# A block with attention, a recurrence, cross-attention and retrieved experts: the last 128 tokens go ahead of the other 384

## The reference

```python
h = rms_norm(x, norm1_g)
qa, ka, va, xl, gl, qc = split(h @ w_in)
o_a = chunk_band_attention(...); o_b = rg_lru_branch(...); o_c = memory_cross_attention(...)
g = sigmoid(h @ w_gate + b_gate)                    # three gates of 2048
x = x + (g0 * (o_a @ wA) + g1 * (o_b @ wB) + g2 * (o_c @ wC)) @ w_o
h = rms_norm(x, norm2_g)
# PEER: 8 heads, each 2 x 128 keys, top 16 of each side, top 16 of the 256 sums
q = h @ w_peer_q;  idx, g = route(q, peer_keys)     # 128 of 16384 experts a token
x = x + sum_k g_k * gelu(peer_u[idx_k] . h) * peer_v[idx_k]
```

## Time and profile before

| | |
|---|---|
| median of 3 runs | 3796.72 us (3788.9 to 3797.24) |
| span of the profiled execution | 3795.8 us (no other time of it is given) |
| TensorE busy | 3763.3 us, 99% |
| VectorE, GpSimd, ScalarE busy | 2360.2, 1701.2, 1259.6 us |
| moved by DMA | 801.10 MB, mean 211 GB/s |

### The profile page before, as it was taken

How to read it: one execution, slowest core, us unless ns; L and a number is a source line. 1 busy time by engine, 2 the same in 40 slices (tenths; PEclk the granted TensorE clock), 3 DMA queues, 4 the chain that set the end, 5 groups by cost and what they waited for, 6 DMA issues and landing times.

```text
span 3795.8 us, 56588 instructions
## 1 busy us (share of the span) xinstructions
PE 3763.3 (99%) x20213; PEld 3454.6 (91%) x20213; DVE 2360.2 (62%) x4031; ACT 1259.6 (33%) x1640; POOL 1701.2 (45%) x1453
## 2 busy tenths in 40 slices
PE   8999999999999999999999999999999999999999
PEld 6778778888888888889999999999999999999999
DVE  5482453000000207886978878888888888888887
ACT  3433453333333323224642222222232222222222
POOL 1444334444444663444025455555544555554222
PEclk9999999999999999999999999999999999999999
DMA  6222112222222323334579889889988898889786
GB/s 209 89 89 101 66 67 89 99 99 92 96 99 99 134 99 109 106 107 147 225 306 328 314 316 343 317 314 335 328 292 294 325 327 312 306 326 338 277 295 226
DMA packets 187962, 801.10 MB, mean 211 GB/s; under 512 B 21024, under 2 KB 59944, under 8 KB 134440
## 3 DMA queue, kind: packets, MB, share of 16 engines
q1 hardware_dynamic: 100864, 492.61, 35.9%
q0 software_dynamic: 83840, 303.09, 22.5%
q10 hardware_dynamic: 3128, 3.88, 0.5%
HBM read 762.39 MB, written 37.09 MB: 211 GB/s over the span
## 4 chain that ended last, share of the span: by engine, by line
PE 88%; DMA 5%; DVE 3%; issue 3%; POOL 1%; ACT 0%; DVEq 0%; POOLq 0%; SPq 0%; ACTq 0%
PE bank L1805 87%; DMA grow<-v_rows,g_col 3%; DMA grow<-u_rows,g_col 2%; DVE w_lo L1625 1%; DVE g_acc L1660 1%; DVE grow L1653 0%; POOL grow L776 0%; DVE xT L1679 0%; DMA ring<-w_exp 0%; PE bank L1982 0%; DMA arena<-mem_t 0%; DVE act_in L1632 0%; DVE act_hi L1636 0%; ACT w_hi L807 0%; POOL w_lo L738 0%
## 5 line engine op out<-in xcount | busy, mean ns | idle before, releaser
L807 ACT ACTIVATE w_hi<-ring 128x1024 fp32r<-128x1024 f32 (+1 forms) x499 | 564.2, 1136 | 1132.8 <-PE bank L1805 612.9
L647 POOL TENSOR_TENSOR p_lo<-ring,p_hi 128x512 fp32r<-128x512 f32 x432 | 563.4, 1305 | 667.4 <-ACT p_hi L807 588.8
L1805 PE MATMUL bank<-h_hi,w_hi 128*128 128x368 f32 (+1 forms) x2304 | 779.9, 338 | 4.7 <-DVE w_lo L1625 3.1
L1805 PE MATMUL bank<-h_hi,w_lo 128*128 128x368 f32 (+1 forms) x2304 | 773.7, 336 | 0.0
L1805 PE MATMUL bank<-h_lo,w_hi 128*128 128x368 f32 (+1 forms) x2304 | 770.8, 336 | 0.0
L1805 PE MATMUL bank<-act_hi,w_hi 128*128 128x368 f32 x2048 | 673.8, 329 | 3.4 <-DVE xT L1679 3.4
L1805 PE MATMUL bank<-act_lo,w_hi 128*128 128x368 f32 x2048 | 673.5, 329 | 0.0
L1805 PE MATMUL bank<-act_hi,w_lo 128*128 128x368 f32 x2048 | 673.5, 329 | 0.0
L776 POOL DMA_INDIRECT grow<-v_rows,g_col x288 | 378.2, 1313 | 537.1 <-DVE g_acc L1660 367.9
L776 POOL DMA_INDIRECT grow<-u_rows,g_col x288 | 365.9, 1270 | 561.4 <-DVE grow L1653 263.4
L1625 DVE TENSOR_TENSOR w_lo<-ring,w_hi 128x1024 fp32r<-128x1024 f32 x448 | 546.4, 1220 | 70.7 <-ACT w_hi L807 47.8
(11 more groups left out here) (226 smaller groups left out, 5077.5 us busy)
## 6 DMA issues: line engine op xcount, KB each, us to landing
ring<-w_exp SPq DMA_DIRECT2D x256, 1024.0 KB
ring<-w_mix SPq DMA_DIRECT2D x64, 1024.0 KB, 4.9
tables<-wt SPq DMA_DIRECT2D x12, 2048.0 KB, 6.5
wg<-tables SPq DMA_DIRECT2D x96, 256.0 KB
ring<-w_qk SPq DMA_DIRECT2D x20, 1024.0 KB, 4.9
ring<-w_o SPq DMA_DIRECT2D x16, 1024.0 KB, 4.8
ring<-w_pq SPq DMA_DIRECT2D x16, 1024.0 KB
xT<-x_t SPq DMA_DIRECT2D x8, 1024.0 KB, 11.9
```

Of the source, the lines that this page charges most:

```text
L647: nc.gpsimd.tensor_tensor(p_lo[:, part, :], ring[slot][:, part, :], p_hi[:, part, :].bitcast(F32), ALU.subtract).then_inc(quarter_lo, 1)
L807: return nc.scalar.activation(out, in_, func, **kw)
L1805: return nc.tensor.matmul(out, lhsT, rhs, start=start, stop=stop)
```

## The change

`NX` goes from 16 to 64, so `ND` from 368 to 320, and the tables from 11 and a half to 10 blocks. The last 128 tokens ("a") go through gates, branch products, merge, output product, second norm, queries, scores and routing first, in 96 parts of 1 MB (64 + 16 + 16), with the tokens as the stationary side and 512 output columns of weights as the moving one. A part is 12 matmuls. Its load takes 2 KB from each row of four tiles. After them the other 384 tokens go through the same weights again, in tiles of 8 KB a row as before, with matmuls of 384 columns. The routing of the early tokens is ranked on VectorE during the first 12 of these tiles; then 110 rows of `u` are gathered beside the tiles (one or two a tile), and 10 more beside the `u` tiles before the tables. In that stage the low parts of quarters 0 and 1 are made by GpSimd and 2 and 3 by VectorE. The rest of the 192 `u` rows and the 192 `v` rows are gathered in the long loop and the tail.

```diff
-NX = 16
+NX = 64
-NTB = TM // TB
+NTB = ND // TB
+A_MIX, A_WO, A_PQ = 64, 16, 16
+A_ALL = A_MIX + A_WO + A_PQ
+QUIET = 12
+B_ROWS = tuple(0 if m < QUIET or m in (63, 64) else 1 if m % 3 == 1 else 2 for m in range(MIX_TILES + KC))
+U1_ROWS = (0, 0, 0, 2, 2, 2, 2, 2)
+U_ROWS = 20
+V_ROWS = 19
...
 SP, before the second pass:
+            def quarter_of(a):
+                part, i = slice(S * (a % 4), S * (a % 4) + S), a // 4
+                if a < A_MIX:
+                    src = mix_of[4 * (i // 4):4 * (i // 4) + 4, i % 4, :, part]
+                else:
+                    w, i = (w_o, i - A_MIX // 4) if a < A_MIX + A_WO else (w_pq, i - (A_MIX + A_WO) // 4)
+                    src = w[4 * i:4 * i + 4, :, part]
+                return src.rearrange("t p n -> p t n")
+            for a in range(A_ALL):
...
+                    sync.wait_ge(a_low, 2 * (a - 2))
+                    sync.wait_ge(a_last, a - 2)
+                sync.dma_start(a_raw[a % 3]..., quarter_of(a)).then_inc(slot_in[a % 3], 16)
...
 ScalarE:
+            def a_high_part(a):
+                act_e.wait_ge(slot_in[a % 3], RINGS + 16 * (a // 3 + 1))
...
+                    act_e.wait_ge(a_done, a - 1)
+                for half in range(2):
+                    part = slice(2 * half, 2 * half + 2)
+                    f(a_hi[a % 2][:, part, :]..., src[:, part]).then_inc(a_high, 1)
...
 VectorE:
+            def a_low_part(a):
+                dve.wait_ge(a_high, 2 * a + 1)
+                v.tensor_tensor(lo[:, 0:2], raw[:, 0:2], hi[:, 0:2].bitcast(F32), ALU.subtract).then_inc(a_low, 1)
+                dve.wait_ge(a_high, 2 * a + 2)
+                v.tensor_tensor(lo[:, 2], raw[:, 2], hi[:, 2].bitcast(F32), ALU.subtract).then_inc(a_low, 1)
...
 GpSimd: the last quarter of each part; then, in the second pass:
+            def early_rows(begin, count):
+                for i in range(begin, begin + count):
+                    for half in range(2):
+                        to = 2 * (i % 2) + half
+                        pool.wait_ge(gath_free, 2 * i + half + 1)
+                        pool.indirect_dma_start(grow[to][:, :], None, half_rows[0],
+                                                bass.IndirectOffsetOnAxis(g_both[:, i, half:half + 1], 0)).then_inc(gath_in[to], 16)
+            for m in range(MIX_TILES + KC):
+                low_quarters(m)
+                if m + 1 < len(B_ROWS):
+                    early_rows(sum(B_ROWS[:m + 1]), B_ROWS[m + 1])
...
+            for j in range(JG):
+                low(R_U1 + j, j % 2)
+                early_rows(N_B + sum(U1_ROWS[:j]), U1_ROWS[j])
...
+            pool.wait_ge(tab_mm, TAB_PARTS)
+            gather_all(0, half_rows[0], g_both, PAIRS, x_both, N_EARLY // 4)
...
 TensorE:
+            def a_part(a, out, of_hi, of_lo, first=0, last=KC - 1, closes=True):
+                for c in range(4):
+                    if c == 0:
+                        pe.wait_ge(a_low, 2 * a + 1)
+                    elif c == 2:
+                        pe.wait_ge(a_low, 2 * a + 2)
+                    elif c == 3:
+                        pe.wait_ge(a_last, a + 1)
+                    k = 4 * (a % 4) + c
+                    ins = split_mm(out, of_hi(k), of_lo(k), a_hi[a % 2][:, c, :], a_lo[a % 2][:, c, :],
+                                   k == first, closes and k == last)
+                ins.then_inc(a_done, 1)
...
+                for t in range(4):       # the bias of a gate, by a diagonal
+                    ins = mm(bank[b][:, P * t:P * t + P], ones[:, :], bias_d[i % 2][:, t, :], start=False, stop=t == 3)
...
-                    ins = split_mm(bank[3 + b][:, :], p_hi[:, n, :], p_lo[:, n, :], branch_hi[n], branch_lo[n],
+                    ins = split_mm(bank[3 + b][:, 0:TM], p_hi[:, n, :], p_lo[:, n, :], mix_hi_b[:, n, :], branch_lo[n][:, 0:TM],
```

More of the change, by code:

```diff
@@ L86 @@
 R_DVE = R_TAB + 1
[L87 removed]
+X_AFTER, EXP_AFTER, ROUTE_AFTER = 5, 5, 6
 BANK_U = (2, 3)
@@ L239, in hybrid_block @@
[L239 to L246, removed]
+        wg = [place("wg", 168, [NTB, JG * TB])[:, :, :], place("wg2", 112, [NTB, JG * TB])[:, :, :]]
+        grow = [place(f"grow{i}", row_at[i], [D // 2]) for i in range(4)]
@@ L687, in _ @@
             fill_low(0)
-            pool.wait_ge(at_a.scores, TT)
+            pool.wait_ge(heads.scores, TT)
             q_stage(2)
@@ new lines, in _ @@
+            for j in range(2):
+                top_pair(j)
+            merge(0)
+            for j in range(2, 4):
+                top_pair(j)
+            row_index()
+            shift_scores()
+            merge(1)
+            dve.wait_ge(tok_copied, 4)
+            done = 0
+            for m in range(QUIET, MIX_TILES):
+                low_quarter(m, 2)
+                first = done
+                if B_ROWS[m]:
+                    a_u_row(done)
+                low_quarter(m, 3)
+                if B_ROWS[m] == 2:
+                    a_u_row(done + 1)
+                done += B_ROWS[m]
+                if m % 4 == 1:
+                    merge((m - 5) // 4)
+                if m == QUIET + 6:
+                    share_scores()
@@ new lines, in _ @@
+            for c in range(KC - 1):
+                merged_low(c)
+            low_quarter(MIX_TILES, 2)
+            merge(KC - 1)
+            low_quarter(MIX_TILES, 3)
+            merged_low(KC - 1)
+            for k in range(1, KC):
+                m = MIX_TILES + k
+                low_quarter(m, 2)
+                if B_ROWS[m]:
+                    a_u_row(done)
+                low_quarter(m, 3)
+                if B_ROWS[m] == 2:
+                    a_u_row(done + 1)
+                done += B_ROWS[m]
+                if k >= 2:
+                    add_x(k - 2)
+                    square(k - 2)
@@ new lines, in _ @@
+            dve.wait_ge(const_made, 4)
+            for q in range(1, 4):
+                part = slice(4 * q, 4 * q + 4)
+                if q < 3:
+                    dve.wait_ge(third_hi, q + 1)
+                else:
+                    dve.wait_ge(split_hi, 3)
+                    dve.wait_ge(second_lo, 4)
+                v.tensor_tensor(w_lo[0][:, part, :], ring[0][:, part, :], w_hi[0][:, part, :].bitcast(F32), ALU.subtract
+                                ).then_inc(third_lo if q < 3 else split_lo, 1)
@@ L2196, in _, with tables @@
             pe.wait_ge(route_copied, 3)
-            def tables(t, b, first, parts=4):
+            def tables(t, b, first):
                 n = 2 * t + b + R_TAB
```

1176 lines of the change are left out of this document (736 added, 440 removed).

## The result

| | before | after |
|---|---|---|
| median | 3794.72 us (3788.9 to 3797.24) | 3887.5 us (3886.38 to 3891.4) |
| ratio, 95% interval | 1 | 1.0247 [1.0233, 1.0262] |
| profiled span | 3795.8 us | 3885.5 us |

The change makes the kernel 2.5% slower; 3692 us were forecast. L numbers are now lines of the changed kernel (and in the experiments lines of each one's own).

The account below looks back on a forecast made before the run. TensorE, busy 99% of the span, was taken as the bound. -244.5 + 15.8 + 5.2 + 37 + 28 + 8 + 20 - 1.1 + 25 + 2 = -104.6 us gave 3692 us, 2.8% faster; 8-in-10 range 3625 to 3800.

Parts of the forecast that it names:

- Dense experts: 256 tiles of 48 matmuls, narrowed from 368 to 320 columns; each matmul saves 19.9 ns: -244.5 us.
- The loop: Long loop of 12 groups of 16 tiles: 2% of 1350 us lost under heavier load, +25 us (0 to +90).
- Rival B: Long loop: VectorE and the gathers become the bound, tiles of 7.4 to 7.7 us, about 3750 to 3810 us; chance 12%.
- Two passes: Gates, output and query products: same columns, but 1,152 more matmuls each paying the rest of 13 ns: +15.8 us.
- First pass at 3.1 us a part: 96 parts of the early tokens, paced nearest to the round of three load buffers: +37 us (bounds +4 and +210).
- Rival C: First pass starves: loads of 2 KB runs at half rate, 5.35 us a part, +216 us, 3908 us; chance 12%.
- Serial places: First pass: start, norm before queries, last merge and change back to tiles, with slow clock after each: +28 us (15 to 45).
- Rival D: First pass: the clock falls to 1.2 GHz, 5.1 us a part, +190 us, 3885 us; chance 3%.
- Second pass beside the rows: 110 row gathers beside tiles of 8.29 us: all engines fit, GpSimd barely, +8 us (0 to +50).
- Rival E: Second pass: GpSimd is late, 68 tiles at 9.0 us, +48 us, 3740 us; chance 5%.
- Eight expert tiles before the tables: The u tiles there: GpSimd's splits stand behind gather issues in five tiles, plus lost clock: +20 us (5 to 30).
- Tables: Table stage: VectorE sets 15.0 us a block; 10 blocks and 6 plain tiles of 7.0 us after: -1.1 us.

Follow-up runs that it names:

- the kernel with the second row later: Changed kernel with nearer gate-weight blocks, VectorE alone on first-pass low parts and early merge; GpSimd issues each tile's second row behind that tile's quarters: 3773.8 us, ratio 0.9955.

## Why the prediction was wrong, point by point

The span rose by 89.7 us where -104.6 was the sum: a miss of 194 us.

- **Dense experts, -244.5: right.** 684 matmuls in 100 us are the 146.2 ns forecast.
- **The loop, +25, and the tail, +2: wrong by 14 us together, in the kernel's favour.** 10,317 matmuls in 1530 us at 146.2 ns are 1508 us, so 22 us were lost in loop and tail; but the kernel before had already lost 15 in 1460, and the +25 was to come on top. From the first matmul of the loop to that of the tail it took 1546.3 us before and 1353.6 after: 192.7 less, where the narrower matmuls alone give 183.4, so the +25 was -9. Tail and end gave back 8 us of the 29 forecast. Rival B didn't come: VectorE 88% and 334 GB/s over the stretch were carried.
- **Two passes, +15.8: right.** Without rows the second pass has 8.34 us a tile against 8.29. The small matmuls, +5.2, were not priced by any run.
- **First pass at 3.1 us a part, +37: wrong by 76 us.** With the serial places it was to last 96 x 3.1 + 28 = 326 us; from its first matmul to that of the second pass it took 402 us (566 to 968). The step that failed is "the DMA engines carried 393 GB/s ... where most packets were under 2 KB": it looked at the size of the pieces and not at where they lie. 44 us come back with nearer blocks. Another 35 come back with VectorE alone on the splits: "VectorE 1.22 and about 0.65 us, and one GpSimd quarter of 1.31 us" were taken as durations side by side, and they lengthen each other. With both edits the marks show 3.20 us a part, and the pass takes 323 us. Rival C had the place, and its threshold (4.2 us a part) was passed by a little, at 4.33 and not at its 5.35; the reason that it gives, short pieces, was not it. The paragraph on the 4 MB between the blocks points to the same rival, at half the rate (196 GB/s); 237 were measured.
- **Serial places, +28: not separable,** but in line with those 323 us. Rival D didn't come: the clock was 0.95 in 600 to 700 us.
- **Second pass beside the rows, +8 (0 to 50): wrong by 120 us,** the largest error. From 968 to 1759 us it took 791 us for 80 tiles, forecast 671; without the rows 121 us come back. The step that failed is "All fit, GpSimd barely ... so a tile can lend to the next". I added each engine's work and compared sums. But the work is in order, and each row ties the engines: GpSimd's quarters stand behind issues that wait for VectorE's products, these stand behind quarters of VectorE's that wait for GpSimd's. Take away either the products or the transfers, and the tile is at 8.35 to 8.45 us. The circle is what these runs leave, together with the waits; of the share that the slower quarter on GpSimd has in it nothing is known. Rival E named GpSimd's lateness, at 9.0 us a tile; over the 68 tiles from the 13th on it was 10.1 ((1759 - 1071) / 68).
- **The merge of the second pass, "a quarter of a merge (0.7)", was priced as work and not by its place.** It stands behind two rows, and ScalarE's next sigmoid, with the high parts behind it, waits for it: 24 us of the above.
- **Eight expert tiles before the tables, +20 (5 to 30): 32 to 35.** The stage took 74.9 us before and 99.8 after, 32 us more than the narrower matmuls would give; without the rows 35 us come back. GpSimd's late splits were there as forecast (21 us of TensorE's waits), but the size was too small, and moving three of the splits away gave nothing, since VectorE was late in its place. The prediction had priced GpSimd alone there.
- **Tables: the pace of a block right, the stage 8 us longer.** Starts of blocks, before and after: 168.3 us for 11 intervals and 138.1 for 9, 15.3 us each in both. But the 16 tiles took 210.1 us before and 201.9 after: 8 us less, where 16.4 (15.3 booked with the dense experts, and the 1.1) were forecast.

```profile
L1587 DVE COPY rst<-arena x12: 240/248/260, 1766.6 to 1934.9; 128x96 f32 x8, 128x96 f32<-128x96 f32 x4
```
```profile
L1994 DVE COPY rst<-arena x10: 242/248/267, 2064.1 to 2202.2; 128x96 f32 x6, 128x96 f32<-128x96 f32 x4
```

76 and 120 us are the miss. The other errors (loop and tail 14 us for the kernel, the stage before the tables 12 and the tables 8 against it, and smaller ones) cancel to within some us, and that is luck. C and E, 12% and 5%, were treated as alternatives, but they lie in different stages, and the losses that they name came both. The range for 8 in 10 left C out and took E in at its own, smaller size.

## What to carry to other kernels

When work of several engines is put side by side, don't compare sums only. Write each engine's queue down in order, mark what each item waits for, and look for a circle: an issue that waits for a product that waits for a split that stands behind the issue. A circle has a period of its own, and work that is small but in a bad place (here a merge of under 3 us) holds up more than its length. Price a load by where its pieces lie, and an elementwise operation by what the other elementwise engine does meanwhile.

## What the hardware showed unexpectedly

- **Blocks 4 MB apart.** Four 2 KB pieces a partition, several loads of 1 MB under way at once: 237 GB/s and 8.6 us from issue to landing at 4 MB, 254 GB/s and 8.0 us at 4 MB + 32 KB, 5.1 us and up to 330 GB/s at 1 MB. The Trainium skill, "DMA: Bandwidth & Descriptors", section "Latency and other measured facts", tells of a slow pitch of 4 MiB between partitions, 103 GB/s, and of 214 with 4 KiB added to the pitch. Here the pitch between partitions is 8 KB, and the loss stands with the distance of the blocks of one partition: 237 GB/s against 287 in the same window with the blocks 1 MB apart. The padding tried here, 32 KB on 4 MB, gave little; 4 KiB was not tried.
- **VectorE and GpSimd.** In these traces an operation of VectorE on two SBUF operands that meets GpSimd's subtraction waits it out. Two single operations in the kernel with the second row later, GpSimd's two quarters and VectorE's half row, which takes 1.22 us alone:

```profile
1199.65 2.52 POOL L814 TENSOR_TENSOR p_lo<-ring,p_hi 128x512 fp32r<-128x512 f32 x2
```
```profile
1199.59 3.67 DVE L1785 SCALAR_TENSOR_TENSOR grow<-grow,h_tok 128x1024 f32<-128x1024 f32 x1 [0.76 <-DMA grow<-u_rows,g_both]
```

1.22 + 2.52 is 3.74, against 3.67. The Trainium skill, "SBUF — State Buffer", section "SBUF: two separate sides", has the rule: a VectorE operation with two SBUF inputs and a GpSimd operation that reads SBUF exclude each other for their whole length. This row agrees; which of the two came first, its stamps, 0.06 us apart, don't settle. Had the prediction used it, the first pass's splits would have been priced one after the other. The indirect issues of GpSimd beside the same products lengthened nothing: 1226 ns in the second pass of the changed kernel.
